# A mixture-of-experts decoder step: list rows dealt eight partitions apart, and one transfer for adjoining blocks of one expert

## The reference, cut to what matters

```
_, eidx = lax.top_k(jnp.where(emask, sel, -jnp.inf), TOP_K)
w = w / jnp.sum(w, axis=-1, keepdims=True) * ROUTED_SCALE
hg = jnp.einsum('td,edf->tef', h, w_gate_e)
hu = jnp.einsum('td,edf->tef', h, w_up_e)
act = jax.nn.silu(hg) * hu * gates[..., None]
routed = jnp.einsum('tef,efd->td', act, w_down_e)
```

## Time and profile before

| | us |
|---|---|
| median of 3 runs (lowest, highest) | 1104.01 (1103.61, 1105.96) |
| the profiled execution's own time | 1104.67 |
| its span in the profile | 1102.8 |
| PE busy | 933.6 (85%) |
| DVE, ACT, POOL busy | 403.8, 201.2, 243.5 |
| q1, q0, q10, share of 16 DMA engines over the span | 57.8%, 12.1%, 0.7% |

### The profile page before, as it was taken

One profiled execution on the slowest core, in us unless ns is written; L12 is line 12 of the kernel. 1 busy time (PEld: TensorE's weight loads), 2 busy tenths in 40 slices (PEclk: granted clock), 3 DMA queues, 4 the chain that ended last, 5 costly groups with the idle time before them and its releaser, 6 DMA issues.

```text
span 1102.8 us, 13691 instructions
## 1 busy us (share of the span) xinstructions
PE 933.6 (85%) x4773; PEld 440.7 (40%) x4773; DVE 403.8 (37%) x975; ACT 201.2 (18%) x414; POOL 243.5 (22%) x301
## 2 busy tenths in 40 slices
PE   4989987987988898689898887997888979998784
PEld 3564555455534554234333332332323324333231
DVE  5947457857773653123212111111111111111116
ACT  6050031041213121111111110111101111111103
POOL 1910029011300166101111111021111220222013
PEclk9989998998989898889999998998989999999898
DMA  9720220232126117989999999999999999999945
GB/s 326 301 77 1 77 77 0 82 84 77 42 77 230 46 55 272 413 341 376 389 382 382 388 396 383 382 379 375 377 381 389 374 374 378 352 346 385 374 143 225
DMA packets 66422, 289.67 MB, mean 263 GB/s; under 512 B 17291, under 2 KB 18539, under 8 KB 41392
## 3 DMA queue, kind: packets, MB, share of 16 engines
q1 hardware_dynamic: 46016, 252.34, 57.8%
q0 software_dynamic: 13232, 35.04, 12.1%
q10 hardware_dynamic: 7104, 1.40, 0.7%
HBM read 257.14 MB, written 41.18 MB: 270 GB/s over the span
## 4 chain that ended last, share of the span: by engine, by line
PE 45%; issue 31%; DVE 12%; ACT 5%; DMA 4%; POOL 2%; SPq 1%; ACTq 0%; POOLq 0%; DVEq 0%
PE bank L986 22%; PE bank L1928 21%; DVE arena L1576 3%; DVE arena L690 2%; DMA sum_rows<-arena 2%; PE bank L1024 2%; POOL expert_lists L492 2%; ACT arena L1249 1%; ACT arena L1236 1%; DMA qkv_samples<-arena 1%; DVE arena L792 1%; DVE bb L712 1%; DMA arena<-in_x_prompt 1%; DVE arena L1907 1%; ACT arena L542 1%
## 5 line engine op out<-in xcount | busy, mean ns | idle before, releaser
L986 PE MATMUL bank<-arena 128*32 128x512 f32 (+6 forms) x2930 | 538.8, 600 | 91.1 <-issue 54.5
L986 PEld LDWEIGHTS bank<-arena 128*32 128x32 f32 (+3 forms) x2930 | 198.9, 132 | 399.4 <-issue 384.2
L1928 PE MATMUL bank<-arena 128*128 128x512 f32 (+9 forms) x1208 | 309.2, 443 | 33.4 <-ACT arena L1533 9.5
L1928 PEld LDWEIGHTS bank<-arena 128*128 128x128 f32 (+4 forms) x1208 | 172.3, 190 | 163.8 <-issue 128.6
L473 POOL DMA_INDIRECT arena<-h_rows,xs x42 | 43.8, 1042 | 466.3 <-DVE bb L712 442.8
L690 DVE SCALAR_TENSOR_TENSOR arena<-arena,xs,bank 128x256 f32<-128x256 f32 x42 | 27.7, 660 | 316.3 <-issue 276.1
L687 DVE COPY arena<-bank 128x512 f32<-128x512 f32 x41 | 28.4, 692 | 176.2 <-PE bank L986 176.2
L482 POOL DMA_INDIRECT sum_rows<-arena,xs x41 | 64.6, 1575 | 58.9 <-DVE arena L687 31.5
L562 ACT ACTIVATE arena<-bank 128x256 f32<-128x256 f32 x42 | 16.1, 384 | 333.5 <-PE bank L986 308.1
L1576 DVE TENSOR_TENSOR arena<-arena 64x512 f32<-64x512 f32 (+8 forms) x79 | 68.3, 865 | 6.6 <-DMA arena<-o_samples 4.0
L492 POOL DMA_INDIRECT expert_lists<-arena,ncim x40 | 40.1, 1003 | 92.4 <-issue 89.2
(11 more groups left out here) (231 smaller groups left out, 528.6 us busy)
## 6 DMA issues: line engine op xcount, KB each, us to landing
arena<-in_w_gate_e SPq DMA_DIRECT2D x64, 1024.0 KB, 20.7
arena<-in_w_up_e SPq DMA_DIRECT2D x64, 1024.0 KB, 34.2
arena<-in_w_down_e SPq DMA_DIRECT2D x64, 1024.0 KB, 34.4
arena<-in_w_in SPq DMA_DIRECT2D x5, 2048.0 KB, 9.0
expert_lists<-arena SPq DMA_DIRECT2D x1, 8482.5 KB, 28.7
arena<-in_x_prompt SPq DMA_DIRECT2D x8, 512.0 KB, 6.6
arena<-in_w_out SPq DMA_DIRECT2D x2, 2048.0 KB, 8.3
sum_rows<-arena SPq DMA_DIRECT2D x8, 512.0 KB, 25.8
```

Of the source, the lines that this page charges most:

```text
L986: return nc.tensor.matmul(o, l, r, start=start, stop=stop, skip_group_check=True)
L1928: return nc.tensor.matmul(o, l, r, start=start, stop=stop, skip_group_check=True, **kw)
```

## The change

It does two things. First, adjoining entries of one rank in a unit become one list transfer (`segments`): three blocks of 32 become one of 96, so a unit of four entries starts two transfers, and the program's list transfers fall from 110 to 74. Second, within such a segment of `width` slots the rows are placed otherwise: slot t holds row `t % 8 * (width // 8) + t // 8` of the segment, so that neighbouring rows of the list are eight partitions apart. The transfer reads its source in that order: an outer loop of width/8 steps (16, 12, 8 or 4) and within each step eight rows that lie width/8 rows apart. The constant `c_unit` says the same to the comparison that finds the empty slots. What is computed does not change.

```
+def segments(u):
+
+    parts = []
+    for r, c0, width, first in UNITS[u]:
+        if parts and parts[-1][0] == r and parts[-1][3] + parts[-1][2] == first:
+            parts[-1] = (r, parts[-1][1], parts[-1][2] + width, parts[-1][3])
+        else:
+            parts.append((r, c0, width, first))
+    return parts
+
+
+def list_row(width, slot):
+
+    return slot % 8 * (width // 8) + slot // 8
+
+
 def lists_landed(u):
 
-    return 16 * sum(len(UNITS[w]) for w in range(u % LISTS, u + 1, LISTS))
+    return 16 * sum(len(segments(w)) for w in range(u % LISTS, u + 1, LISTS))
...
-            for r, c0, width, first in UNITS[u]:
+            for r, c0, width, first in segments(u):
                 e = act.value_load(order_i[0:1, r:r + 1], min_val=0, max_val=NE - 1)
                 act.dma_start(lists[u % META][c0:c0 + width, :],
-                              tab_list[bass.ds(e, 1), first:first + width, :].rearrange("a c w -> (a c) w")
+                              tab_list[bass.ds(e, 1), first:first + width, :].rearrange("a (n m) w -> m (a n) w", n=8)
                               ).then_inc(s(f"list{u % LISTS}"), 16)
...
     for u, tiles in enumerate(UNITS):
+        for r_, c0, width, first in segments(u):
+            unit[c0:c0 + width, u] = [first + list_row(width, t_) for t_ in range(width)]
         for r_, c0, width, first in tiles:
-            unit[c0:c0 + width, u] = first + np.arange(width)
             unit[c0:c0 + width, 64 + u] = TT * ACCS[u][r_] - FAR
```

## The result

The changed kernel takes 1111.95 us (median of 4, 1110.68 to 1113.84), where before took 1104.99 beside it (median of 4). The ratio is 1.0069 (95% interval 1.0053 to 1.0084): slower by 0.7%. Measured once more beside other experiments, it was 1.0103 (1.0085 to 1.0122).

The account below looks back on a forecast made before the run. The busiest DMA engine was taken to set the units' stage's end. Terms 1 + 4.5 + 2 = +7.5 us on 1104.67 gave 1112.2, or 1111.5 us as median; range 1107.5 to 1117, widened down to 1103.5 for the first rival.

Parts of the forecast that it names:

- The bound: Units' stage: bound by transfers, its end set by the busiest DMA engine, as the share dwindles before the last weights land.
- The 0.253 us of a row: Gathers and scatters in the units' stage: each 4 KB row takes its DMA engine 0.253 us.
- Part 1: Gathered and scattered rows: the busiest engine goes from 330 rows to 335, costing +1 us (0 to 2.5).
- The dealing of four and four: Gathers and scatters: an engine serves four neighbouring slots in each half of 64, such as 0 to 3 and 32 to 35.
- Part 2: List transfers: as many engines as outer-loop steps, so some carry 536 rows for 302, costing +4.5 us.
- 6012 packets: List queue: the count expected if lists travel on 16, 12, 8 or 4 engines; 6528 would mean 16 engines.
- Part 3: Start of the units' stage: the first lists land later than the 7.1 us of cover allows, costing +2 us (0 to 5).
- Part 4: ACT's queue and later lists: 36 fewer list transfers, later landings and the constant table change nothing.
- Lists on 16 engines: Rival on list transfers: they still use all 16 engines, so 1104.4 us, no change; chance 0.22.
- Eight neighbours on an engine: Rival on gathers and scatters: eight neighbouring slots share an engine, rows even out, 30 us gained, 1074 us; chance 0.05.
- the landings at 35.0 us: Sign on down weights: landings far below 34.9 us after issue would show the load evened out and the forecast wrong.
- Late engines served faster: Rival on the units' stage: engines running ahead leave memory to the late ones, 17 us gained, 1094.5 us; chance 0.05.

Follow-up runs that it names:

- halves: The changed kernel with neighbouring slots taking rows from the two halves of a list, not its eighths: 1094.4 us, ratio 0.9919 to before.
- quarters: The changed kernel with neighbouring slots taking rows from the four quarters of a list, not its eighths: 1081.72 us, ratio 0.9806 to before.
- eighths: The changed kernel itself, its stride of width/8 against the kernel before: 1111.95 us, ratio 1.0069; measured again 1113.64 us, 1.0103.
- first lists whole: The changed kernel with the first four units' lists in the old row order: 1110.54 us, ratio 1.0059 to before; measured again 1109.8 us, 1.0075.
- merging alone: The changed kernel with the old order of rows, adjoining blocks still one transfer: 1103.55 us, ratio 1.0001 to before.
- second copies: Merging alone, plus each list from the fifth unit on fetched again in eighths into four unread tiles: 1113.49 us; with one tile and a ScalarE wait, 1138.74 us.
- Sixteenths: The changed kernel with sixteenths of a list for eighths: 1128.67 us, ratio 1.0228; with the first four units' lists in old order, 1121.52 us.

## Why the prediction was right

1111.5 us was forecast and 1111.95 measured; the sum was +7.5, and the two measurements give 0.69% and 1.03% of some 1103 us, +7.6 and +11.4. The direction and the mechanism hold, and the sum is at the low end. That it met the first measurement within 0.5 us is luck: the second lies 4 us higher, and two of the terms below are known only within 3 us.

**The bound.** That the busiest DMA engine sets the stage's end was read from a share that dwindles. The strides show it: same bytes, and 572.5 to 612.6 us of stage. The 0.253 us of a row hold as well, for a row that is gathered and scattered twice that: 20 rows fewer on the fullest engine (halves) are 10.1 us, measured 8.4 to 10.2 in the stage against its 593.1 and 594.9 without a stride; 48 fewer (quarters) are 24.3 less some 1 for lists, measured 20.6 to 22.4. The rows of each engine are worked out, not seen in a view.

**Part 1 (+1, 0 to 2.5).** The dealing of four and four, read from 15 rows of one scatter, is confirmed by the halves' gain and the eighths' loss, and with it that eighths put rows of the front half of every list on the same engines. Its size stays open. With the first lists whole, the stage takes 601.2 us (two traces: 601.3 and 601.1) for 594.0 (before and merging alone, 594.9 and 593.1): +7.2 for rows and lists together. Less the 5.9 that the lists cost by the stage, 1.3 are left for the rows. By the medians it is 7.1 and 7.9 less 3.0, so 4 to 5. The sum had 1 (0 to 2.5), which may have been too small. The prediction counted the fullest engine alone, 330 and 335 rows. But by the same dealing two engines had over 320 rows before, and eight have after; the weights' queue ahead of the last product shows five engines at work for three. Weights that wait for the last of eight engines, in place of two, would cost more; that was only argued. The old order on few engines wasn't tried: a list in one piece is one run of rows and goes on 16.

**Part 2 (+4.5).** Right in mechanism; the size lies between +3.0 and +5.9, by the second copies. 6012 packets were predicted and 6012 counted. Quarters have 32, 24, 16 and 8 runs in the four widths; on 16, 12, 16 and 8 engines these are 9 x 16 + 18 x 12 + 30 x 16 + 17 x 8 = 976 reports, and with 5344 rows 6320 packets, as its page of the profile has it:

```profile
q10 hardware_dynamic: 6320, 1.39, 0.6%
```

Sixteenths have 5678, for 8, 6, 4 and 2 engines, and halves 6528, for 16 throughout.
The rule is that of the Trainium skill's page "DMA: Bandwidth & Descriptors", section "Why a DMA increments its semaphore by 16 and not by 1" (the largest number of engines up to 16 that divides the outermost dimension of both patterns); these packet counts agree with it.

**Part 3 (+2, 0 to 5).** Right in time and in size, but partly by luck, since the way was another. Forecast was the third list 463.5 to 468 us in before's time, 21.6 to 26.1 after the first issue; it came after 22.8 (460.27 us, since this run was earlier). The prediction took the seven issues as alike before and after. Not foreseen: ScalarE needs 12.79 us instead of 7.53 for them, which makes a part of that lateness and holds up PE on a way of its own, 6.4 of the 8.7 us by which PE's last shared transposes are late. Nor was it foreseen that of the 4.5 us by which the copy behind the transposes is late (469.95 - 437.47 = 32.5 for 28.0), 2.6 are given back at once. The first unit's product takes 7.09 us for 9.74. PE was idle for 0.98 us ahead of it, for 7.93 before, and the granted clock in 470 to 480 us is 1.00, the upper level of 2.4 GHz throughout, where the row of before has 0.69, a mean of the two levels:

```profile
470.75 9.74 PE L986 MATMUL bank<-arena 128*64 128x512 f32 x32 [7.93 <-DVE arena L678]
```

```profile
470.83 7.09 PE L1002 MATMUL bank<-arena 128*64 128x512 f32 x32 [0.98 <-DVE arena L694]
```

```profile
470.00:480.00 10.00, 9.25 (x32) 3.17 (x32) 0.60 (x1) 0.49 (x1) 0.00 (x0) 0.69 0.86 358
```

The first trace is of before, the second of the changed kernel, the third of before again. 1.9 us remain to the first product, and some 2 more are lost in the stage. The way there is another than the prediction named: it held that the late first unit frees its weight slots late; but already the sixth expert's weights, into a slot that is free, stand on SP behind the shared sums' stores and go out 11 us later, and the engines run dry at once. What is queued on SP behind the late work was not followed far enough.

**Part 4 (nothing).** Merging alone: 1.0001. Right. The later lists stay covered too: from 490 to 1070 us VectorE waits for them 0.9 us, in two waits.

**The rivals.** Lists on 16 engines: excluded by 6012 packets. Eight neighbours on an engine: excluded by the landings at 35.0 us, the share that still dwindles, the halves, and the change's own loss. Late engines served faster: the stage would have become shorter; it became 8.2 us longer, and the down weights land no earlier.

## What to carry to other kernels

When gathers and scatters have empty slots, the DMA engines don't share the rows evenly, and a stage at a DMA share of 1.00 can still be bound by one engine: look at how the share falls off ahead of the stage's last landing, and place full and empty slots so that each engine gets both. The right stride is that of the dealing (here four neighbours, and quarters gained 1.9%); a stride of twice that lost 0.7 to 1.0%: it sorted the rows by engine once more, so that the fullest engine stayed as full (335 rows for 330), and what it did to the lists came on top. A transfer whose outer loop has few steps runs on few engines: count its packets, time its issue, and keep such patterns away from the transfers that the first work of a stage waits for.

## What was not expected of the hardware

ScalarE's time to issue a transfer depends on the pattern. The median of the first seven list issues (line 396) is 476 ns for a list in one piece, 548 for quarters, but 1092 for eighths and 1027 for sixteenths; together they take 7.52, 8.20, 12.79 and 12.87 us:

```profile
L396 ACTq DMA_DIRECT2D prm<-expert_lists x7: 370/476/584, 438.4 to 445.6; - x7
```

```profile
L396 ACTq DMA_DIRECT2D prm<-expert_lists x7: 547/548/689, 437.4 to 445.0; - x7
```

```profile
L396 ACTq DMA_DIRECT2D prm<-expert_lists x7: 598/1092/1251, 437.5 to 449.7; - x7
```

These are merging alone, quarters and the change. What makes eighths dear and quarters not was left open. It matters here because ScalarE's own copies, and through them PE, stand behind these issues.

A list of 65 words a row is 1.2% of the DMA time, yet a second copy of it on few engines cost 10 us, 0.9% of the kernel, in a stage with a DMA share of 1.01. And one wait of ScalarE for such a copy cost 25 us more (1138.74 for 1113.49), with the same transfers but for the tile that the second copies land in.
